# The low part of each mixer's last output chunk on VectorE, two reordered steps at the end of the RWKV mixer, and an arena 224 bytes lower

## Chip, core and metric

The kernel runs on one core of a Trainium2 chip. The metric is the device time of one launch in microseconds (us). The kernel before takes 1237.35 us (median of three runs, 1236.31 to 1237.88). Its profiled execution took 1236.65 us, of which 1234.8 us are the span that the profile covers.

The engines are named as in the profile: PE is TensorE, PEld its weight load, DVE is VectorE, ACT is ScalarE, POOL is GpSimd, SP issues the DMAs of the weights.

## What is computed

The reference is two transformer blocks on 256 tokens of width 1024, all in float32. Four SwiGLU feed-forward layers of width 2816 alternate with three mixers:

```python
x = x + 0.5 * swiglu(rmsnorm(x, ffn1_norm), gate, up, down)                # ffn 0
x = x + concat([spatial_gating(...), gated_delta_rule(...)]) @ w_out       # mix1
x = x + 0.5 * swiglu(rmsnorm(x, ffn2_norm), gate, up, down)                # ffn 1
x = rmsnorm(x, final_norm)
x = x + concat([forgetting_attention(...), causal_pool(...)]) @ hy_w_out   # fox
x = x + swiglu(rmsnorm(x), gate, up, down)                                 # ffn 2
x = x + (group_norm(rwkv7_scan(...)) + bonus) * g @ rw_w_o                 # rwkv
x = x + swiglu(rmsnorm(x), gate, up, down)                                 # ffn 3
```

Each mixer ends in a product of a 256 x 1024 activation with a 1024 x 1024 weight (`w_out`, `hy_w_out`, `rw_o`), added to the residual `x`. What follows is a feed-forward layer, whose first step is the norm of that sum.

## The kernel before

**Weights.** All weights come as a stream of chunks of 128 x 2048 float32 (1 MB each), in the order of their use. SP loads chunk c into `raw[:, c % 3]`. For products that are split in three, ScalarE rounds the chunk to `whi` (`high`, line 314) and GpSimd makes the rest, `wlo = raw - whi` (`low`, line 3371); both have three slots. TensorE then runs three passes of float32r products: high by high, high by low, low by high (`three_passes`, lines 341 to 346), or in the feed-forward layers one product of 512 columns and one of 256 (`ffn_tile`, lines 353 and 355). The semaphores are `high_made`, `low_made` (one more for each chunk) and `chunk_used`. `LOWS[c]` is the count that `low_made` has once the chunk c has its low part. GpSimd works through the lows strictly in the order of the stream, with a few other tasks in between.

**The arena.** Apart from the weights, `x` and constants, nearly everything lies in one buffer, `arena`; `f_both` (the feed-forward's activations, high and low), `hhi`, `hlo`, `key_hi`, `key_lo` are names for places in it. It starts behind a filler, `up_to_line`.

**The end of a mixer.** An output weight is four chunks of 256 columns. Chunks 0 and 1 are multiplied together (512 columns to a product, `pair_tiles`), then chunk 2 and chunk 3 alone in `last_out` (48 products of 256 columns each). Between them TensorE transposes pieces of the new `x` for the next norm (`turn_piece`, line 750). Chunk 3 can be rounded by ScalarE only when the pair is done, since it takes a slot that the pair used; its low part follows on GpSimd. VectorE adds the products to `x` in four steps (`add_out`, lines 1039 to 1045), and after the second has nothing to do until the first transposed piece has been rounded (`low_piece`, line 692).

**The end of the RWKV mixer.** Its output Y (kept where `x` was; `x` itself is saved in `kept_x` and comes back by DMA, line 2479) is finished in four passes w = 0 to 3, two token halves by two halves of the width. For each pass VectorE runs `normed(w)`, `whole(w)` (line 2755) and `gated(w)` (line 2764); TensorE transposes the result (`turned(w)`, line 3209); ScalarE rounds it to `hhi` (`y_high`, line 2475); VectorE makes `hlo` (`y_low(w)`, line 2770), which TensorE's `out_tiles(w)` waits for: 4 tiles by three passes, 12 products of 512 columns. The order of each engine is written out by hand. GpSimd makes the low part of `rw_o` chunk 2 only after the last `y_low` (it waits for `rw_ylo` at 4).

Of the kernel before, what the change touches and what calls it, by code (L numbers as in the profile page):

```python
# [20 lines left out]
P = 128  # L21
# [3 lines left out]
KT = D // P  # L25
# [3 lines left out]
RAW = 3  # L29
# [3 lines left out]
F32 = mybir.dt.float32  # L33
F32R = mybir.dt.float32r
ALU = mybir.AluOpType
# [158 lines left out]
def build(nc, stream, consts, vectors, x_in, rows, kept_x, out):  # L194
    names = stream_plan(STAGES)
    CH = {name: c for c, name in enumerate(names)}
# [14 lines left out]
    with ctx:  # L211
        def sb(name, shape, dt=F32):
            return ctx.enter_context(nc.sbuf_tensor(name, shape, dt))
# [12 lines left out]
        stat = sb("stat", [P, 64])  # L226
        sb("up_to_line", [P, 72])
        H_AT = 23040
# [456 lines left out]
        def pieces_vector(eng, n, stage, factor):  # L685
# [10 lines left out]
            def first_low(c, j):  # L696
# [4 lines left out]
                if j == 3:  # L701
                    eng.wait_ge(s("first_low"), 4 * c + 4)
                    nc.vector.tensor_copy(stat[:, 58:59], stat[:, 62:63]).then_inc(low_made, 1)

            for j in range(4):
                if stage:
                    add_out(eng, OUT_KIND[STAGES[stage - 1][0]], j)
                    if j:
                        low_piece(j - 1)
                else:  # L710
                    low_piece(j)
                    first_low(0, j)
# [333 lines left out]

        PAIR_BANKS = {"w_out": (3, 7), "hy_w_out": (6, 7), "rw_o": (5, 6)}
        LAST_BANKS = {"w_out": (6, 7), "hy_w_out": (0, 6), "rw_o": (0, 6)}

# [1474 lines left out]
        def rwkv_vector(eng, st):  # L2524
# [304 lines left out]
            normed(3)  # L2829
            whole(3)  # L2830
            y_low(2)
            gated(3)
            y_low(3)
            eng.wait_ge(s("x_kept"), 48)

        def rwkv_tensor(eng, st):
# [374 lines left out]

            def out_tiles(w):

                m, q = PASSES[w]
                eng.wait_ge(s("rw_ylo"), w + 1)
                return pair_tiles("rw_o", range(4 * q, 4 * q + 4), 0, m, last=KT - 1)

# [19 lines left out]
            out_tiles(0)  # L3237
            out_tiles(1)
            turned(2)
            turned(3)  # L3240
            out_tiles(2)
# [118 lines left out]
        def _(pool):  # L3360
# [13 lines left out]
            def lows_ffn(c0):  # L3374

                for c in range(c0, c0 + 3):
                    if c >= 2:
                        low(c)
                with pool.Fori(0, GROUPS - 1) as i:
                    for r in range(3):  # L3380
                        low(c0 + 3 + r, i)
# [3 lines left out]
            for st in STAGES:  # L3385
# [3 lines left out]
                while c < NCH and names[c][0] not in ("gate", "up", "down"):  # L3389
# [4 lines left out]
                    if c == CH[("rw_o", 0, 0)]:  # L3394
                        rwkv_pool(pool, low)
                    elif c not in PLAIN and names[c] not in (("lora", 0, 2), ("rw_o", 0, 1)):
                        low(c)
# [78 lines left out]
```

## Time and profile before

| | us |
|---|---|
| time, median of three runs | 1237.35 (1236.31 to 1237.88) |
| profiled execution | 1236.65 |
| its span | 1234.8 |
| PE busy | 1221.0 (99%) |
| POOL busy | 776.7 (63%) |
| ACT busy | 608.5 (49%) |
| DVE busy | 538.0 (44%) |

A row of a timeline gives the start and the length in us, the engine, the line, the operation, what it writes from what, and in brackets how long the engine had been idle before and what ended that. A product's length includes its way through the array, so the pace of TensorE is the distance between two starts, not the length.

### The profile page before, as it was taken

Reading aid. Unit: us, or ns where it says so; the run is one execution under the profiler, and the core shown is the slowest. Engines: PE = TensorE matmul, PEld = TensorE weight load, DVE = VectorE, ACT = ScalarE, POOL = GpSimd, SP = SyncE. Lnnn points to the kernel's source line nnn. Section 1 sums busy time; section 2 is a strip of 40 time slices with the busy share of each in tenths; the row PEclk is TensorE's granted clock in tenths of the full one; section 3 lists DMA queues with packets and bytes.
Section 4 is the critical chain, followed back from the end, with each engine's and each line's share of the span. In section 5 each row is a group of like instructions: output and inputs, shape, how many; then the busy total and the mean of one; then the engine's idle time right before and its main releaser. Section 6 shows DMA issues by size and latency. Waiting matters only on the chain.

```text
span 1234.8 us, 23237 instructions
## 1 busy us (share of the span) xinstructions
PE 1221.0 (99%) x9698; PEld 1062.6 (86%) x9698; DVE 538.0 (44%) x819; ACT 608.5 (49%) x796; POOL 776.7 (63%) x200
## 2 busy tenths in 40 slices
PE   8999999999999999999999999999999999999998
PEld 7888887788988888899898888888888998888887
DVE  4432234655333333343523333348986573332233
ACT  7454443545554444585565445464422444554442
POOL 3988880153288888767369888843016525888884
PEclk9999999999999999999999999999999999999999
DMA  8655554253255555554235555542341133555551
GB/s 301 212 186 199 178 201 148 89 184 140 103 174 201 202 175 200 193 184 160 103 137 202 176 201 179 195 170 103 136 163 44 38 117 122 184 195 197 180 201 68
DMA packets 31020, 202.01 MB, mean 164 GB/s; under 512 B 3424, under 2 KB 5344, under 8 KB 7392
## 3 DMA queue, kind: packets, MB, share of 16 engines
q1 hardware_dynamic: 28064, 196.63, 45.2%
q10 hardware_dynamic: 2880, 4.26, 1.0%
q8 instruction: 60, 0.98, 0.3%
q14 instruction: 16, 0.13, 0.0%
HBM read 198.79 MB, written 2.10 MB: 163 GB/s over the span
## 4 chain that ended last, share of the span: by engine, by line
PE 95%; ACT 1%; POOL 1%; issue 1%; DVE 1%; DMA 1%; SPq 0%; POOLq 0%; DVEq 0%; ACTq 0%
PE psum L353 25%; PE psum L355 13%; PE psum L344 10%; PE psum L346 10%; PE psum L345 10%; PE psum L986 6%; PE psum L999 3%; PE psum L2992 2%; PE psum L3008 1%; POOL wlo L3371 1%; PE psum L2847 1%; PE psum L341 1%; PE psum L343 1%; PE psum L342 1%; PE psum L2962 1%
## 5 line engine op out<-in xcount | busy, mean ns | idle before, releaser
L3371 POOL TENSOR_TENSOR wlo<-raw,whi 128x2048 fp32r<-128x2048 f32 x160 | 734.3, 4595 | 289.7 <-ACT whi L314 244.3
L353 PE MATMUL psum<-f_both,whi 128*128 128x512 f32 x1408 | 497.3, 394 | 1.0 <-DVE wlo L699 1.0
L314 ACT ACTIVATE whi<-raw 128x2048 fp32r<-128x2048 f32 x160 | 306.3, 1915 | 223.1 <-PE psum L355 173.9
L355 PE MATMUL psum<-f_both,wlo 128*128 128x256 f32 x1408 | 397.4, 282 | 0.0
L353 PEld LDWEIGHTS psum<-f_both,whi 128*128 128x128 f32 x1408 | 264.4, 188 | 62.0 <-DVE wlo L699 1.6
L355 PEld LDWEIGHTS psum<-f_both,wlo 128*128 128x128 f32 x1408 | 264.7, 188 | 1.5
L344 PE MATMUL psum<-whi,ahi 128*128 128x512 f32 x352 | 137.2, 390 | 0.2 <-POOL wlo L3371 0.2
L346 PE MATMUL psum<-whi,alo 128*128 128x512 f32 x352 | 137.0, 389 | 0.0
L345 PE MATMUL psum<-wlo,ahi 128*128 128x512 f32 x352 | 137.0, 389 | 0.0
L909 DVE TENSOR_TENSOR psum<-psum,arena 128x512 f32<-128x512 f32 x43 | 30.1, 700 | 239.7 <-ACT arena L625 239.6
L925 DVE TENSOR_TENSOR alo<-arena,ahi 128x512 fp32r<-128x512 f32 x44 | 98.7, 2244 | 31.7 <-ACT ahi L858 31.7
L916 DVE TENSOR_TENSOR psum<-psum,arena 128x512 f32<-128x512 f32 x44 | 30.8, 700 | 174.5 <-ACT arena L625 174.5
L344 PE MATMUL psum<-whi,hhi 128*128 128x256 f32 (+1 forms) x328 | 100.1, 305 | 0.4 <-POOL wlo L3371 0.2
L346 PE MATMUL psum<-whi,hlo 128*128 128x256 f32 (+1 forms) x328 | 97.4, 297 | 0.0
L345 PE MATMUL psum<-wlo,hhi 128*128 128x256 f32 (+1 forms) x328 | 97.4, 297 | 0.0
L344 PEld LDWEIGHTS psum<-whi,ahi 128*128 128x128 f32 x352 | 66.1, 188 | 14.5 <-POOL wlo L3371 0.5
L346 PEld LDWEIGHTS psum<-whi,alo 128*128 128x128 f32 x352 | 66.0, 188 | 13.7
L345 PEld LDWEIGHTS psum<-wlo,ahi 128*128 128x128 f32 x352 | 66.1, 188 | 12.2
L986 PE MATMUL psum<-arena,raw 128*128 128x256 f32 x320 | 73.9, 384 | 0.8 <-issue 0.8
L986 PEld LDWEIGHTS psum<-arena,raw 128*128 128x128 f32 x320 | 59.3, 190 | 10.4 <-issue 2.7
L344 PEld LDWEIGHTS psum<-whi,hhi 128*128 128x128 f32 x328 | 62.0, 189 | 4.6 <-issue 1.6
L345 PEld LDWEIGHTS psum<-wlo,hhi 128*128 128x128 f32 x328 | 62.2, 190 | 1.9
(425 smaller groups left out, 1474.1 us busy)
## 6 DMA issues: line engine op xcount, KB each, us to landing
raw<-stream SPq DMA_DIRECT2D x182, 1024.0 KB, 4.8
con<-consts SPq DMA_DIRECT2D x1, 1376.0 KB, 14.2
x<-x_in SPq DMA_DIRECT2D x1, 1024.0 KB, 4.9
raw<-stream SPq DMA_DIRECT2D x2, 512.0 KB, 6.9
kept_x<-x ACTq DMA_DIRECT2D x1, 1024.0 KB, 3.9
x<-kept_x ACTq DMA_DIRECT2D x2, 512.0 KB, 4.7
out<-x SPq DMA_DIRECT2D x4, 256.0 KB, 2.0
arena<-gm_w_s ACTq DMA_DIRECT2D x1, 512.0 KB
```

The source lines that it names most:

```text
L314: nc.scalar.activation(whi[:, slot, :], raw[:, c % RAW, :], ACT.Copy).then_inc(high_made, 1)
L344: nc.tensor.matmul(out, h_hi, w_hi, start=start, stop=False, skip_group_check=skip)
L345: nc.tensor.matmul(out, h_hi, w_lo, start=False, stop=False, skip_group_check=skip)
L346: return nc.tensor.matmul(out, h_lo, w_hi, start=False, stop=stop, skip_group_check=skip)
L353: nc.tensor.matmul(psum[:, bank, :].rearrange("p (a n) -> p a n", a=2), whi[w], f_both[:, :, k, :], start=k == 0, stop=False, skip_group_c ...
L355: return nc.tensor.matmul(psum[:, bank, 0:TOK], wlo[w], f_hi[:, k, :], start=False, stop=k == KT - 1, skip_group_check=True)
L909: nc.vector.tensor_tensor(left, left, aside[:, 0, :, :], ALU.add).then_inc(s("ffn_sum"), 1)
L916: nc.vector.tensor_tensor(left, left, aside[:, 1, :, :], ALU.add).then_inc(s("ffn_sum"), 1)
L925: nc.vector.tensor_tensor(flat(alo), act[:, b, :], flat(ahi).bitcast(F32), ALU.subtract)\
L986: mm = nc.tensor.matmul(psum[:, bank, j * 256:(j + 1) * 256], raw[:, slot, k * 256 + j * P:k * 256 + j * P + P], h[:, k, :], start=k == 0, ...
L999: mm = nc.tensor.matmul(psum[:, bank, m * 256:m * 256 + n], h[:, k, m * P:m * P + P], raw[:, slot, k * 256:k * 256 + n], start=k == 0, sto ...
L3371: nc.gpsimd.tensor_tensor(part(wlo[:, slot, :]), part(raw[:, c % RAW, :]), part(whi[:, slot, :]).bitcast(F32), ALU.subtract)\
```

## The change

There are three parts.

1. The filler before the arena has 16 columns instead of 72. The arena, and all that lies in it, starts 56 x 4 = 224 bytes lower in each partition: at byte 103968 instead of 104192. 104192 is 407 x 256; 103968 is 406 x 256 + 32. What lies before the filler stays where it was.
2. The low part of chunk 3 of `w_out`, `hy_w_out` and `rw_o` is made by VectorE (`last_out_low`), between the second and the third residual addition. GpSimd leaves these three out, and before its first low of the feed-forward layer that follows it waits until `low_made` has counted VectorE's. It waits in the first feed-forward layer for nothing.
3. At the end of the RWKV mixer `gated(3)` stands ahead of `y_low(2)` on VectorE, and `turned(2)` stands in the middle of `out_tiles(1)` on TensorE instead of behind it.

```diff
--- before.py
+++ after.py
@@ -224,7 +224,7 @@
         con = sb("con", [P, CONSTS.shape[1]])
         vec = sb("vec", [P, VEC_COLS])
         stat = sb("stat", [P, 64])
-        sb("up_to_line", [P, 72])
+        sb("up_to_line", [P, 16])
         H_AT = 23040
         MORE_AT = H_AT + 2 * KT * TOK
         ARENA = MORE_AT + 3072
@@ -702,9 +702,18 @@
                     eng.wait_ge(s("first_low"), 4 * c + 4)
                     nc.vector.tensor_copy(stat[:, 58:59], stat[:, 62:63]).then_inc(low_made, 1)
 
+            def last_out_low(c):
+                slot = SLOT[c]
+                eng.wait_ge(high_made, LOWS[c] - 2)
+                eng.wait_ge(low_made, LOWS[c] - 1)
+                nc.vector.tensor_tensor(wlo[:, slot, :], raw[:, c % RAW, :], whi[:, slot, :].bitcast(F32), ALU.subtract)\
+                    .then_inc(low_made, 1)
+
             for j in range(4):
                 if stage:
                     add_out(eng, OUT_KIND[STAGES[stage - 1][0]], j)
+                    if j == 1:
+                        last_out_low(CH[(OUT_KIND[STAGES[stage - 1][0]], 0, 3)])
                     if j:
                         low_piece(j - 1)
                 else:
@@ -1045,6 +1054,7 @@
                 nc.vector.tensor_tensor(xs, xs, bank2(LAST_BANKS[kind][j - 2]), ALU.add).then_inc(x_ready, 1)
 
         PAIR_BANKS = {"w_out": (3, 7), "hy_w_out": (6, 7), "rw_o": (5, 6)}
+        LAST_CHUNKS = [(kind, 0, 3) for kind in ("w_out", "hy_w_out", "rw_o")]
         LAST_BANKS = {"w_out": (6, 7), "hy_w_out": (0, 6), "rw_o": (0, 6)}
 
         def pair_slots(kind):
@@ -2828,8 +2838,8 @@
             gated(2)
             normed(3)
             whole(3)
+            gated(3)
             y_low(2)
-            gated(3)
             y_low(3)
             eng.wait_ge(s("x_kept"), 48)
 
@@ -3209,11 +3219,11 @@
                     mm = nc.tensor.transpose(bank4(GATE_BANK[w])[:, k, :], Y[:, m, (4 * q + k) * P:(4 * q + k + 1) * P], const("ident"))
                 mm.then_inc(s("rw_out"), 1)
 
-            def out_tiles(w):
+            def out_tiles(w, tiles=range(4)):
 
                 m, q = PASSES[w]
                 eng.wait_ge(s("rw_ylo"), w + 1)
-                return pair_tiles("rw_o", range(4 * q, 4 * q + 4), 0, m, last=KT - 1)
+                return pair_tiles("rw_o", [4 * q + k for k in tiles], 0, m, last=KT - 1)
 
             u_from_state(2)
             state_and_next_values(2)
@@ -3235,8 +3245,9 @@
             for j in range(2):
                 eng.wait_ge(low_made, LOWS[CH[("rw_o", 0, j)]])
             out_tiles(0)
-            out_tiles(1)
+            out_tiles(1, (0, 1))
             turned(2)
+            out_tiles(1, (2, 3))
             turned(3)
             out_tiles(2)
             out_tiles(3).then_inc(chunk_used, 2)
@@ -3373,6 +3384,8 @@
 
             def lows_ffn(c0):
 
+                if c0:
+                    pool.wait_ge(low_made, LOWS[c0] - 1)
                 for c in range(c0, c0 + 3):
                     if c >= 2:
                         low(c)
@@ -3393,7 +3406,7 @@
                         mix1_pool(pool, (3,))
                     if c == CH[("rw_o", 0, 0)]:
                         rwkv_pool(pool, low)
-                    elif c not in PLAIN and names[c] not in (("lora", 0, 2), ("rw_o", 0, 1)):
+                    elif c not in PLAIN and names[c] not in (("lora", 0, 2), ("rw_o", 0, 1)) and names[c] not in LAST_CHUNKS:
                         low(c)
                     c += 1
 
```

VectorE at the end of the RWKV mixer, before (line 2755 is `whole`, 2764 `gated`, 2770 `y_low`, 1039 and 1045 `add_out`, 692 `low_piece`):

```order
L2751 TENSOR_TENSOR x<-x,arena 128x512
L2755 TENSOR_TENSOR x<-x,arena 128x512
L2770 TENSOR_TENSOR hlo<-psum,hhi 128x4x128
L2764 TENSOR_TENSOR x<-x,psum 128x512
L2770 TENSOR_TENSOR hlo<-psum,hhi 128x4x128
L1039 TENSOR_TENSOR x<-x,psum 128x2x256 x2
L692 SCALAR_TENSOR_TENSOR f_both<-psum,vec,f_both 128x256 x2
L1045 TENSOR_TENSOR x<-x,psum 128x2x256
```

and after (ten lines further down in the file: 2765, 2774, 2780; the new operation is line 709):

```order
L2761 TENSOR_TENSOR x<-x,arena 128x512
L2765 TENSOR_TENSOR x<-x,arena 128x512
L2774 TENSOR_TENSOR x<-x,psum 128x512
L2780 TENSOR_TENSOR hlo<-psum,hhi 128x4x128 x2
L1048 TENSOR_TENSOR x<-x,psum 128x2x256 x2
L709 TENSOR_TENSOR wlo<-raw,whi 128x2048
L692 SCALAR_TENSOR_TENSOR f_both<-psum,vec,f_both 128x256 x2
L1054 TENSOR_TENSOR x<-x,psum 128x2x256
```

The gating of the last pass has moved ahead of both remaining `y_low`, and the new `wlo<-raw,whi` stands between the additions of output chunks 0 and 1 and the first `low_piece`.

TensorE from the second tile of `out_tiles(1)` to the beginning of `out_tiles(2)`, before (lines 344 to 346 are the three passes of one tile; 3209 is `turned`, four transposes each):

```order
L344 MATMUL psum<-whi,hhi 128x512
L345 MATMUL psum<-wlo,hhi 128x512
L346 MATMUL psum<-whi,hlo 128x512
L344 MATMUL psum<-whi,hhi 128x512
L345 MATMUL psum<-wlo,hhi 128x512
L346 MATMUL psum<-whi,hlo 128x512
L3209 MATMUL psum<-con,x 128x128 x8
L344 MATMUL psum<-whi,hhi 128x512
```

and after (`turned` is line 3219):

```order
L344 MATMUL psum<-whi,hhi 128x512
L345 MATMUL psum<-wlo,hhi 128x512
L346 MATMUL psum<-whi,hlo 128x512
L3219 MATMUL psum<-con,x 128x128 x4
L344 MATMUL psum<-whi,hhi 128x512
L345 MATMUL psum<-wlo,hhi 128x512
L346 MATMUL psum<-whi,hlo 128x512
L344 MATMUL psum<-whi,hhi 128x512
L345 MATMUL psum<-wlo,hhi 128x512
L346 MATMUL psum<-whi,hlo 128x512
L3219 MATMUL psum<-con,x 128x128 x4
L344 MATMUL psum<-whi,hhi 128x512
```

The eight transposes stood together behind all four tiles of pass 1; now four of them, those of pass 2, have two tiles (six products) between them and those of pass 3.

VectorE at the end of mix1, where `w_out`'s additions are four narrower instructions (line 1042 before, 1051 after), after the change:

```order
L1547 TENSOR_TENSOR hlo<-arena,hhi 128x512
L1051 TENSOR_TENSOR x<-x,psum 128x256 x4
L709 TENSOR_TENSOR wlo<-raw,whi 128x2048
L692 SCALAR_TENSOR_TENSOR f_both<-psum,vec,f_both 128x256 x2
L1054 TENSOR_TENSOR x<-x,psum 128x2x256
```

The new operation has the same place there, as it has behind `hy_w_out`.

## Rows read from the trace of the kernel before

**Rows 1.** The page, first part: busy us (share of the span) xinstructions of each engine.

```profile
PE 1221.0 (99%) x9698; PEld 1062.6 (86%) x9698; DVE 538.0 (44%) x819; ACT 608.5 (49%) x796; POOL 776.7 (63%) x200
```

**Rows 2.** PE timeline, RWKV out_tiles(0) to the first product of chunk 2: start, length.

```profile
1018.14 0.48 PE L344 MATMUL psum<-whi,hhi 128*128 128x512 f32 x1
...
1023.81 0.60 PE L3209 MATMUL psum<-con,x 128*128 128x128 f32 x4
1026.48 0.66 PE L3209 MATMUL psum<-con,x 128*128 128x128 f32 x4 [2.08 <-DVE x L2764]
1026.90 0.47 PE L344 MATMUL psum<-whi,hhi 128*128 128x512 f32 x1
...
1034.12 0.28 PE L344 MATMUL psum<-whi,hhi 128*128 128x256 f32 x1
```

**Rows 3.** Window: us, busy (x) of PE, PEld, DVE, ACT, POOL; PEclk, DMA, GB/s.

```profile
1026.90:1034.12 7.22, 7.22 (x28) 5.76 (x26) 0.69 (x1) 0.69 (x2) 4.58 (x1) 0.76 0.24 75
```

**Rows 4.** DVE timeline at the same place.

```profile
1020.79 0.69 DVE L2764 TENSOR_TENSOR x<-x,psum 128x512 f32<-128x512 f32 x1
...
1022.35 0.69 DVE L2755 TENSOR_TENSOR x<-x,arena 128x512 f32<-128x512 f32 x1
1025.14 0.69 DVE L2770 TENSOR_TENSOR hlo<-psum,hhi 128x512 fp32r<-128x512 f32 x1 [2.11 <-ACT hhi L2475]
1025.75 0.68 DVE L2764 TENSOR_TENSOR x<-x,psum 128x512 f32<-128x512 f32 x1
```

**Rows 5.** ACT queue at the same place: the second half of x comes back.

```profile
1027.18 0.33 ACTq L2479 DMA_DIRECT2D x<-kept_x  x1
```

**Rows 6.** The line that brings x back: its DMAs from issue to landing.

```profile
DMA to landing us min/median/max: 4.6/4.7/4.8
```

**Rows 7.** POOL timeline, low parts of rw_o chunks 2 and 3.

```profile
1028.65 4.58 POOL L3371 TENSOR_TENSOR wlo<-raw,whi 128x2048 fp32r<-128x2048 f32 x1 [28.50 <-DVE hlo L2770]
1036.39 4.59 POOL L3371 TENSOR_TENSOR wlo<-raw,whi 128x2048 fp32r<-128x2048 f32 x1 [3.17 <-ACT whi L314]
```

**Rows 8.** PE timeline around the start of rw_o chunk 3.

```profile
1039.82 1.03 PE L750 MATMUL psum<-con,x 128*128 128x128 f32 x8
1041.04 0.39 PE L344 MATMUL psum<-whi,hhi 128*128 128x256 f32 x1 [0.18 <-POOL wlo L3371]
```

**Rows 9.** DVE timeline, additions of rw_o chunks 0 and 1.

```profile
1034.38 1.29 DVE L1039 TENSOR_TENSOR x<-x,psum 128x512 f32<-128x512 f32 x2 [5.88 <-PE psum L346]
```

**Rows 10.** Line 2628, a low part made by VectorE: ns, min/median/max.

```profile
L2628 DVE TENSOR_TENSOR wlo<-raw,whi x1: 1212/1212/1212, 913.2 to 913.2; 128x1024 fp32r<-128x1024 f32 x1
```

**Rows 11.** Groups by line: shapes, count, busy us, mean ns of one, idle before.

```profile
L925 DVE TENSOR_TENSOR alo<-arena,ahi 128x512 fp32r<-128x512 f32 x44 | 98.7, 2244 | 31.7 <-ACT ahi L858 31.7
```

**Rows 12.** PE timeline, end of hy_w_out chunk 2 and start of chunk 3.

```profile
632.22 1.03 PE L750 MATMUL psum<-con,x 128*128 128x128 f32 x8
633.01 0.37 PE L344 MATMUL psum<-whi,hhi 128*128 128x256 f32 x1
```

**Rows 13.** POOL timeline at that place: low of hy_w_out chunk 3.

```profile
627.36 4.61 POOL L3371 TENSOR_TENSOR wlo<-raw,whi 128x2048 fp32r<-128x2048 f32 x1 [3.18 <-ACT whi L314]
```

**Rows 14.** DVE timeline there: additions of hy_w_out chunks 0 and 1.

```profile
626.73 1.28 DVE L1039 TENSOR_TENSOR x<-x,psum 128x512 f32<-128x512 f32 x2 [9.64 <-PE psum L346]
```

**Rows 15.** PE timeline in the first feed-forward layer: a wait, then full clock.

```profile
10.17 0.50 PE L353 MATMUL psum<-f_both,whi 128*128 128x512 f32 x1 [1.04 <-DVE wlo L699]
```

**Rows 16.** The window around it, all engines, columns as in rows 3.

```profile
9.00:15.00 6.00, 4.96 (x28) 4.13 (x28) 5.76 (x13) 6.00 (x14) 0.00 (x0) 1.00 1.03 437
```

**Rows 17.** Groups by line of PE: products streamed from the arena and from whi.

```profile
L353 PE MATMUL psum<-f_both,whi 128*128 128x512 f32 x1408 | 497.3, 394 | 1.0 <-DVE wlo L699 1.0
...
L344 PE MATMUL psum<-whi,ahi 128*128 128x512 f32 x352 | 137.2, 390 | 0.2 <-POOL wlo L3371 0.2
...
L345 PE MATMUL psum<-wlo,hhi 128*128 128x256 f32 x288 | 81.0, 281 | 0.0
...
L342 PE MATMUL psum<-hlo,whi 128*128 128x256 f32 x48 | 13.5, 282 | 0.0
```

## The prediction

> **What bounds the kernel now.** I read the first part of the page first: TensorE is busy 1221.0 us, 99% of the span, and no other engine is above 63% [rows 1]. So an edit on VectorE or GpSimd is worth only what TensorE waits for it, and the question for each of the three parts is whether TensorE waits at that place. I then read TensorE's timeline at the ends of the three mixers, which the change touches, and the timelines of VectorE, ScalarE and GpSimd beside it.
>
> There is one wait worth speaking of. In the RWKV mixer TensorE finishes `out_tiles(1)` and `turned(2)`, which starts at 1023.81, and then stands idle for 2.08 us until `turned(3)` starts at 1026.48; VectorE's line 2764, the gating, ended it [rows 2]. VectorE's timeline says why: `whole(3)` starts at 1022.35 and takes 0.69, and `gated(3)` could follow at once, but `y_low(2)` stands ahead of it in the queue and waits for ScalarE until 1025.14; `gated(3)` runs at 1025.75 [rows 4]. TensorE thus waits for something that stands behind an operation which needs TensorE's own last result.
>
> This wait has a second price. `out_tiles(0)` and `out_tiles(1)`, 24 products, take 1023.81 - 1018.14 = 5.67 us. The same number in `out_tiles(2)` and `(3)` takes 1034.12 - 1026.90 = 7.22 us [rows 2]. In the window of those 7.22 us the granted clock is 0.76 on average [rows 3], so TensorE was for a part of it at 1.2 GHz instead of 2.4, after the idle stretch. That cost 7.22 - 5.67 = 1.55 us.
>
> A second, small wait is in front of `rw_o` chunk 3. TensorE starts eight transposes at 1039.82 and the chunk at 1041.04, on GpSimd's low part [rows 8]. At the end of `hy_w_out` the same eight transposes take 633.01 - 632.22 = 0.79 us with no wait behind them [rows 12]. So 1.22 - 0.79 = 0.43 us were lost there.
>
> **The reordering (part 3), step by step.** `turned(2)` needs `gated(2)`, done at 1020.79 + 0.69 = 1021.48 [rows 4]. It now starts after 18 of the 24 products: 1018.14 + 18 x 0.236 = 1022.39, no wait. Four transposes take 0.42 (1026.48 to 1026.90). Six more products end at 1024.23. `gated(3)` now starts right behind `whole(3)`, 1022.35 + 0.72 = 1023.07, and is done by 1023.75, so `turned(3)` starts at 1024.23 without a wait, and `out_tiles(2)` could start at 1024.65. It needs `y_low(2)`. Before, `y_low(2)` started 1.33 after `turned(2)` (1023.81 to 1025.14), ScalarE's rounding included; now that gives 1022.39 + 1.33 = 1023.72, and `gated(3)` is out of VectorE's way by then; it ends at 1024.41, 0.24 before it is wanted. So the 2.08 us go, and `out_tiles(2)` starts at 1024.65 instead of 1026.90: 2.25 us. If the clock stays up, the 24 products take 5.67 and end at 1030.32 instead of 1034.12: 3.80 us in all.
>
> What is late next is GpSimd. Its low part of `rw_o` chunk 2 starts only after the last `y_low`; before, that was 1028.65, 2.17 after `turned(3)`, and it took 4.58 [rows 2, 7]. Now 1024.23 + 2.17 = 1026.40, done at 1030.98, seen by TensorE some 0.05 later, as with chunk 3 (1036.39 + 4.59 = 1040.98 against 1041.04 [rows 7, 8]). TensorE arrives at 1030.32 and waits 0.7 us, until 1031.03. Of the 3.80 us 3.09 stay.
>
> The saved `x` comes back by a DMA that is issued behind the last rounding, at 1027.18, 0.70 after `turned(3)` [rows 5]; it takes up to 4.8 us [rows 6]. Now it is issued at 1024.93 and lands by 1029.7. VectorE's first addition comes 0.26 after the pair's last product (1034.38 against 1034.12 [rows 2, 9]), now 1030.58. It is not late.
>
> **The low part of chunk 3 on VectorE (part 2).** The trace has the same operation on VectorE at half the width, 1.21 us for 1024 columns [rows 10], so I take 2.4 us for 2048, against 4.6 on GpSimd [rows 7]. In the RWKV mixer ScalarE's rounding was ready when GpSimd began, 1036.39 - 1034.12 = 2.27 after the pair; now 1032.59. The two additions, 1.29 us [rows 9], are done at 1031.87. So the low part is ready at about 1035.0. TensorE wants it at 1031.03 + 5.70 (chunk 2, 1034.12 to 1039.82) + 0.79 = 1037.52. The wait of 0.43 us is gone, with 2.5 us to spare.
>
> At `hy_w_out` nothing was waited for before, so nothing can be won. The rounding is ready at 627.36 [rows 13], the additions end at 626.73 + 1.28 = 628.01 [rows 14], the low part would be ready at 630.4, and TensorE wants it at 633.01 [rows 12]. It is behind 2.6 us of slack. `w_out` is laid out alike. Nothing: 0.
>
> The operation stands on VectorE ahead of `low_piece(0)`, which waits for transposes that start only at 1039.82 [rows 8], 4.2 us after the additions are done (1034.38 + 1.29 [rows 9]); these idle microseconds hide it. GpSimd's new wait holds back the low of the first feed-forward chunk; what is queued behind it there is only the feed-forward's lows. Before, that chunk had to wait for GpSimd's 4.6 us of chunk 3 anyway; VectorE is done earlier than that, so the new wait costs nothing as long as VectorE takes under 4.6 us.
>
> VectorE and GpSimd do disturb each other here. Line 925 reads two operands from the arena and `ahi` and takes 2244 ns for 512 columns [rows 11], while the half-chunk above took 1212 ns for 1024 [rows 10]. The Trainium skill, page "SBUF — State Buffer", section "Who interferes with whom", says that a VectorE instruction with two SBUF inputs and a GpSimd instruction that reads SBUF exclude each other for their whole length; the slow row fits it. It would speak against moving this very kind of operation to VectorE. Its result is a rival below.
>
> **The arena (part 1).** No row of before shows a product that streams from an address 32 bytes past a multiple of 64, so its cost has to be bounded. The products that stream from `f_both` in the arena take 394 ns each, 1408 of them; those that stream as many columns from `whi`, outside it, 390 [rows 17]. If the place of the start were behind these 4 ns, the move could give them back or cost as much again: 1408 x 4 ns = 5.6 us either way. The other pair says that it does not matter: 256 columns streamed from `hlo` in the arena take 282 ns, from `wlo` outside it 281 [rows 17], at different distances from a multiple of 256. That is the nearer pair, since it differs in the place alone; I take 0. The Trainium skill, same page, section "Operand start alignment", asks only for a multiple of the element's size, and says that this is about what is allowed and that nothing was timed; it leaves the sum as it is.
>
> **The sum.** 3.09 + 0.43 + 0 + 0 = 3.52 us. The profiled execution takes 1236.65, of which 1234.8 are the span; with the change it would be 1233.1. The median of the runs shown is 0.70 above the profiled one, so I predict 1237.35 - 3.5 = 1233.8 us. Its own range, from waits of some tenths at the splits, is 1233.0 to 1234.9.
>
> **Rivals.**
> 1. *The new wait for GpSimd takes the clock down as the old one did.* For it: TensorE still stands for 0.7 us before chunk 2. Against: in the first feed-forward layer TensorE stood for 1.04 us [rows 15] and the granted clock around it is 1.00 [rows 16]. It would cost the 1.55 us again: 1235.3. Chance 8%.
> 2. *The arena's place slows the streaming products.* A mechanism of its own: a start off a line costs each of the 1408 pairs of products something. From 2.5 ns on it eats the gain; at 4 ns, 5.6 us, the time is 1239.4, slower than before; to be slower by more than can be told it takes 4.3 ns. For it: lines 353 and 344 do differ by 4 ns. Against: the pair of 281 and 282 ns. 16%.
> 3. *The arena's place makes them faster.* The same 4 ns won: 1228.2. For and against as above. 10%.
> 4. *VectorE's low part meets GpSimd.* If it ran at the pace of line 925, 4 x 2.24 = 9.0 us, it would end at 1032.59 + 9.0 = 1041.6, 4.1 us after TensorE wants it, and at 628.01 + 9.0 = 637.0, 4.0 us late, at `w_out` about the same: 12 us lost against 3.5 won, 1246. It decides from about 5 us on. This is what the rule on the shared port would do. Against: GpSimd's next low waits on this very operation, and its low of chunk 2 ends (1030.98) before the rounding is ready (1032.59). 3%.
> 5. *The reordering does not bring what it says*: `y_low(2)` becomes the thing that is late, since it now stands behind `gated(3)`, and TensorE stands for it instead; if the 2.08 us and the slow clock only moved there, the 0.43 us would be all that is won: 1236.9. Against: the 0.24 us of slack worked out above. 3%.
>
> The forecast has 60%. A measurement of this kernel tells about 0.2% from no change, 2.5 us; 3.5 is not far above it, so I count one in eight of the forecast as "same". Faster: 0.53 of the forecast and 0.09 of rival 3, 0.62. Slower: 0.08 of rival 2, 0.03 of rival 4 and 0.03 for what I do not see, 0.14. Same: the rest, 0.24. The range is 1230.0 to 1239.0: it leaves out the far halves of rivals 2 and 3, and rival 4.
>
> **What would show it.** In the profile after: TensorE's wait on the gating gone, and a new one of 0.3 to 1.0 us on GpSimd's line before `rw_o` chunk 2; four transposes after 18 products; 24 products of `out_tiles(2)` and `(3)` in about 5.7 us at a granted clock of 1.00; VectorE's low part three times at 2.2 to 2.6 us, and no wait before chunk 3. Lines 353 and 355 with the same mean and the feed-forward layers of the same length would show that the arena's place is nothing. The prediction is wrong if these layers change in length, if the clock falls again, or if VectorE's new operation takes over 4.6 us.

## The result: 1229.66 us, and the profile after

The changed kernel takes 1229.66 us (median of six runs, 1229.11 to 1231.06), the kernel before 1236.76 beside it (six runs, 1235.15 to 1237.88). The ratio is 0.9944, with a 95% interval of 0.9931 to 0.9957. That is 7.1 us, twice the 3.5 of the forecast and below its range, which ended at 1230.0. The profiled execution of the changed kernel has a span of 1227.9 us against 1234.8.

I cut both traces at the first and the last product of line 353 of each feed-forward layer. The distances between these rows, after minus before:

| stretch | before | after | difference |
|---|---|---|---|
| start to the first product of ffn 0 | 10.17 | 10.62 | +0.45 |
| ffn 0 | 174.46 | 173.47 | -0.99 |
| mix1 | 157.68 | 158.49 | +0.81 |
| ffn 1, 2 and 3, each | 173.03 | 171.78 | -1.25 (-3.75 for the three) |
| fox | 123.81 | 124.28 | +0.47 |
| rwkv | 235.01 | 231.06 | -3.95 |

They sum to -6.96; the spans differ by 6.9. The feed-forward layers gave 4.74 us that were not forecast, and inside them the change moves nothing but the address of their operand. Of the RWKV mixer's 3.95 us, 3.34 lie behind the first product of `out_tiles(0)`: from there to the first product of ffn 3 it is 1041.48 - 1015.77 = 25.71 us instead of 1047.19 - 1018.14 = 29.05, near the forecast. The other 0.6 us lie ahead of it, in a part where profiles differ by up to 2.4 us without any rule that I could find.

**The end of the RWKV mixer.** TensorE's timeline after the change, from the first product of `out_tiles(0)` to the start of chunk 3 (the lines are the same as in [rows 2, 8]; `turned` is 3219 now and `turn_piece` 759):

```profile
1015.77 0.47 PE L344 MATMUL psum<-whi,hhi 128*128 128x512 f32 x1
...
1020.05 0.60 PE L3219 MATMUL psum<-con,x 128*128 128x128 f32 x4
...
1021.89 0.60 PE L3219 MATMUL psum<-con,x 128*128 128x128 f32 x4
1022.24 0.48 PE L344 MATMUL psum<-whi,hhi 128*128 128x512 f32 x1
...
1027.69 0.39 PE L346 MATMUL psum<-whi,hlo 128*128 128x512 f32 x1
1028.65 0.39 PE L344 MATMUL psum<-whi,hhi 128*128 128x256 f32 x1 [0.56 <-POOL wlo L3382]
...
1034.51 1.03 PE L759 MATMUL psum<-con,x 128*128 128x128 f32 x8
1035.30 0.36 PE L344 MATMUL psum<-whi,hhi 128*128 128x256 f32 x1
```

Read the distances from the first row: `turned(2)` comes 4.28 behind it (forecast 4.25), `turned(3)` 6.12 (6.09), `out_tiles(2)` 6.47 (6.51), chunk 2 12.88 (12.89), and chunk 3 another 6.65 behind chunk 2 (6.49). No wait stands at either `turned`. The one that is left is on GpSimd, before chunk 2: 0.56 us. The window of that stretch (columns as in [rows 3]) shows that the clock stayed up:

```profile
1017.65:1028.65 11.00, 10.44 (x50) 8.13 (x49) 5.38 (x10) 2.45 (x5) 4.60 (x1) 1.00 0.15 49
```

VectorE's timeline at the same place shows the gating (2774) straight behind `whole` (2765), both `y_low` (2780) behind it, and the new low part (709):

```profile
1019.98 0.69 DVE L2765 TENSOR_TENSOR x<-x,arena 128x512 f32<-128x512 f32 x1
1020.70 0.69 DVE L2774 TENSOR_TENSOR x<-x,psum 128x512 f32<-128x512 f32 x1
1021.32 0.69 DVE L2780 TENSOR_TENSOR hlo<-psum,hhi 128x512 fp32r<-128x512 f32 x1
1023.16 0.69 DVE L2780 TENSOR_TENSOR hlo<-psum,hhi 128x512 fp32r<-128x512 f32 x1 [1.14 <-ACT hhi L2485]
1028.19 1.28 DVE L1048 TENSOR_TENSOR x<-x,psum 128x512 f32<-128x512 f32 x2 [4.34 <-PE psum L346]
1030.15 2.29 DVE L709 TENSOR_TENSOR wlo<-raw,whi 128x2048 fp32r<-128x2048 f32 x1 [0.68 <-ACT whi L314]
```

The low part takes 2.29 us and is done at 1032.44; TensorE wants it at 1035.30. GpSimd, one operation shorter, does these two here:

```profile
1023.99 4.60 POOL L3382 TENSOR_TENSOR wlo<-raw,whi 128x2048 fp32r<-128x2048 f32 x1 [26.77 <-DVE hlo L2780]
1032.86 4.62 POOL L3382 TENSOR_TENSOR wlo<-raw,whi 128x2048 fp32r<-128x2048 f32 x1 [4.27 <-ACT whi L314]
```

**The feed-forward layers.** The groups of TensorE by line, of the changed kernel, which answer to [rows 17]:

```profile
L353 PE MATMUL psum<-f_both,whi 128*128 128x512 f32 x1408 | 492.2, 393 | 1.9 <-DVE wlo L699 1.9
L355 PE MATMUL psum<-f_both,wlo 128*128 128x256 f32 x1408 | 393.7, 280 | 0.0
L344 PE MATMUL psum<-whi,ahi 128*128 128x512 f32 x352 | 137.4, 390 | 0.3 <-POOL wlo L3382 0.3
...
L345 PE MATMUL psum<-wlo,hhi 128*128 128x256 f32 x288 | 81.0, 281 | 0.0
```

The same view of the kernel before has this for line 355:

```profile
L355 PE MATMUL psum<-f_both,wlo 128*128 128x256 f32 x1408 | 397.4, 282 | 0.0
```

The mean lengths moved by 1 or 2 ns, and the products of lines 344 and 345 did not move. It is the pace that tells. Eight neighbouring products of line 353 in ffn 1, before:

```profile
512.18 0.40 PE L353 MATMUL psum<-f_both,whi 128*128 128x512 f32 x1
512.41 0.28 PE L355 MATMUL psum<-f_both,wlo 128*128 128x256 f32 x1
...
514.64 0.39 PE L353 MATMUL psum<-f_both,whi 128*128 128x512 f32 x1
...
515.34 0.40 PE L353 MATMUL psum<-f_both,whi 128*128 128x512 f32 x1
```

and after, where the first row is that of the layer's first product:

```profile
342.58 0.48 PE L353 MATMUL psum<-f_both,whi 128*128 128x512 f32 x1
...
511.93 0.39 PE L353 MATMUL psum<-f_both,whi 128*128 128x512 f32 x1
512.16 0.28 PE L355 MATMUL psum<-f_both,wlo 128*128 128x256 f32 x1
...
514.36 0.39 PE L353 MATMUL psum<-f_both,whi 128*128 128x512 f32 x1
```

Seven pairs of products take 514.64 - 512.18 = 2.46 us before and 514.36 - 511.93 = 2.43 after. Over all pairs the mean from the start of a 353 to that of its 355 fell from 230.7 to 229.5 ns, and from a 355 to the next 353 from 120.0 to 117.5: 3.7 ns a pair. 1408 pairs times 3.7 ns is 5.2 us; the layers lost 4.7. The last rows of the two fences are the last products of the layer: 515.34 - 342.31 (its first, before) = 173.03 and 514.36 - 342.58 = 171.78.

So two questions were open: is it the arena that does this, by what property of its address, and what are the other two parts worth by themselves?

### The profile page after: what moved, and what is told of

Its sections match the earlier page's. It is cut to its first block, busy times and chain, and to the rows that moved or that the text cites. A ratio compares the mean times of both kernels' runs of the same rounds, so it can differ in the third digit from the quotient of the medians.

```text
span 1227.9 us, 23243 instructions
## 1 busy us (share of the span) xinstructions
PE 1214.9 (99%) x9698; PEld 1059.2 (86%) x9698; DVE 540.9 (44%) x822; ACT 608.6 (50%) x796; POOL 765.3 (62%) x197
## 4 chain that ended last, share of the span: by engine, by line
PE 95%; ACT 1%; POOL 1%; issue 1%; DVE 1%; DMA 1%; SPq 0%; POOLq 0%; DVEq 0%
PE psum L353 25%; PE psum L355 13%; PE psum L344 10%; PE psum L346 10%; PE psum L345 10%; PE psum L995 6%; PE psum L1008 3%; PE psum L3002 2%; PE psum L3018 1%; POOL wlo L3382 1%; PE psum L2857 1%; PE psum L341 1%; PE psum L342 1%; PE psum L343 1%; PE psum L2972 1%
## 5 line engine op out<-in xcount | busy, mean ns | idle before, releaser
L3382 POOL TENSOR_TENSOR wlo<-raw,whi 128x2048 fp32r<-128x2048 f32 (+1 forms) x157 | 722.9, 4608 | 295.5 <-ACT whi L314 210.0
L353 PE MATMUL psum<-f_both,whi 128*128 128x512 f32 x1408 | 492.2, 393 | 1.9 <-DVE wlo L699 1.9
L355 PE MATMUL psum<-f_both,wlo 128*128 128x256 f32 x1408 | 393.7, 280 | 0.0
L934 DVE TENSOR_TENSOR alo<-arena,ahi 128x512 fp32r<-128x512 f32 x44 | 94.4, 2146 | 31.7 <-ACT ahi L867 31.7
L867 ACT ACTIVATE ahi<-arena 128x512 fp32r<-128x512 f32 x44 | 27.9, 633 | 73.8 <-DVE arena L931 73.8
```

Source lines behind the costliest of these rows:

```text
L353: nc.tensor.matmul(psum[:, bank, :].rearrange("p (a n) -> p a n", a=2), whi[w], f_both[:, :, k, :], start=k == 0, stop=False, skip_group_c ...
L355: return nc.tensor.matmul(psum[:, bank, 0:TOK], wlo[w], f_hi[:, k, :], start=False, stop=k == KT - 1, skip_group_check=True)
L934: nc.vector.tensor_tensor(flat(alo), act[:, b, :], flat(ahi).bitcast(F32), ALU.subtract)\
L3382: nc.gpsimd.tensor_tensor(part(wlo[:, slot, :]), part(raw[:, c % RAW, :]), part(whi[:, slot, :]).bitcast(F32), ALU.subtract)\
```

## The three parts, each by itself

**The arena alone.** The kernel before with one number changed:

```diff
-        sb("up_to_line", [P, 72])
+        sb("up_to_line", [P, 16])
```

> Part 1 alone: the filler has 16 columns, all else as before. Theory A (the arena's place sets the pace of the products that stream from it): the feed-forward layers shorten from 173.03 us to 171.78 us each, as in the changed kernel, 4.7 to 5 us in all; mix1 and fox lengthen by 0.8 and 0.5 us if their lengthening is the place's too; the time is 3.5 us under before. Theory B (the place is nothing, and the layers are shorter because GpSimd and VectorE share the work in another way): the layers stay at 173.03 and the time stays within 0.5 us of before.

Measured: 1232.68 us, ratio 0.9972 (0.9962 to 0.9983). This and the next three runs are compared with the kernel before as it ran beside them, 1236.36 us. The layers take 173.48 once and 171.78 three times, as in the changed kernel (173.47 and 171.78); the groups of lines 353 and 355 read 492.2 and 393.7 us, as there. The arena is the cause in the feed-forward layers, and it is worth 0.28% in all, 3.5 us. Fox gave back 0.5 us of it: 124.31 here against 123.81 before, and 123.81 to 123.95 in the next three runs, which have the old arena. Mix1's 157.93 is not the arena's doing: the next two runs have 157.90 and 157.94 with the arena where it was (before 157.68).

This run showed something on the side. The old wait at `turned(3)` is there, and the clock did not fall. Its timeline of TensorE and the window behind the wait:

```profile
1024.93 0.66 PE L3209 MATMUL psum<-con,x 128*128 128x128 f32 x4 [2.08 <-DVE x L2764]
1025.35 0.48 PE L344 MATMUL psum<-whi,hhi 128*128 128x512 f32 x1
...
1031.76 0.39 PE L344 MATMUL psum<-whi,hhi 128*128 128x256 f32 x1 [0.56 <-POOL wlo L3371]
```

```profile
1024.00:1031.00 7.00, 6.07 (x28) 4.82 (x28) 1.57 (x3) 0.69 (x2) 3.91 (x1) 1.00 0.22 77
```

The same 2.08 us as in [rows 2], but a granted clock of 1.00 behind it instead of 0.76 [rows 3]; and TensorE, not slowed, met the wait on GpSimd that the slow stretch had hidden. Chunk 2 starts 15.17 us behind the first product of `out_tiles(0)`, against 15.97 before. The fallen clock cost 0.80 us at the end, not 1.55.

**The reordering alone** (`gated(3)` ahead of `y_low(2)`, and `turned(2)` after two of the four tiles):

```diff
-            y_low(2)
             gated(3)
+            y_low(2)
...
-            out_tiles(1)
+            out_tiles(1, (0, 1))
             turned(2)
+            out_tiles(1, (2, 3))
```

> Part 3 alone: gated(3) ahead of y_low(2), turned(2) in the middle of out_tiles(1); filler 72, low parts all on GpSimd. By the forecast's steps 3.1 us less: the wait of 2.08 us and the slow clock gone, a wait of 0.6 to 0.7 us for GpSimd before rw_o chunk 2, and the small wait before chunk 3 (0.43 us) still there or changed by some tenths. Feed-forward layers at 173.03. Rival: the reordering gives the whole gain of 7 us; then the layers would be at 171.78 here.

Measured: 1233.83 us, ratio 0.9978 (0.9969 to 0.9987): 0.22% of 1236.36, 2.7 us. Chunk 2 starts 12.84 behind the first product, 3.13 sooner than before and 2.33 sooner than in the run with the clock up. GpSimd and TensorE at chunk 3:

```profile
1034.26 13.75 POOL L3372 TENSOR_TENSOR wlo<-raw,whi 128x2048 fp32r<-128x2048 f32 x3 [1.61 <-ACT whi L314]
```

```profile
1038.57 1.04 PE L750 MATMUL psum<-con,x 128*128 128x128 f32 x8
1039.36 0.37 PE L344 MATMUL psum<-whi,hhi 128*128 128x256 f32 x1
```

The first of the three lows is that of chunk 3: 1034.26 + 4.6 = 1038.9, before TensorE arrives at 1039.36. The 0.43 us of [rows 8, 12] is gone with the reordering alone: TensorE, made to wait for GpSimd before chunk 2, does not meet it again before chunk 3.

**VectorE's low part alone** (`last_out_low` and its wait in `lows_ffn`, as in the diff of the change; order and filler as before):

```diff
                     add_out(eng, OUT_KIND[STAGES[stage - 1][0]], j)
+                    if j == 1:
+                        last_out_low(CH[(OUT_KIND[STAGES[stage - 1][0]], 0, 3)])
```

> Part 2 alone: chunk 3's low part on VectorE in all three mixers, filler 72, order as before. Forecast: 0.4 us less, from the wait before rw_o chunk 3, nothing elsewhere. Theory B expects the feed-forward layers at 171.78 and 3 to 4 us less. If the lengthening of mix1 (0.8) and fox (0.5) comes from VectorE's operation, it is seen here.

Measured: 1236.78 us, ratio 1.0003 (0.9994 to 1.0012). Nothing. In its profile the wait before chunk 3 is gone (6.48 us from chunk 2 to chunk 3, against 6.92), and the clock had fallen again behind the old wait:

```profile
1027.69 0.66 PE L3219 MATMUL psum<-con,x 128*128 128x128 f32 x4 [2.08 <-DVE x L2774]
1028.10 0.47 PE L344 MATMUL psum<-whi,hhi 128*128 128x512 f32 x1
```

```profile
1028.10:1035.30 7.20, 7.20 (x27) 5.73 (x26) 0.69 (x1) 0.69 (x2) 4.58 (x1) 0.76 0.22 75
```

0.44 us is 0.04% and lies inside the interval; and in a run where the clock stays up, as with the arena alone, TensorE meets GpSimd before chunk 2 and its trace has no wait before chunk 3 that could be removed.

**Both of these without the arena** (the changed kernel with the old filler):

```diff
-        sb("up_to_line", [P, 16])
+        sb("up_to_line", [P, 72])
```

> Parts 2 and 3 together, filler 72: what the forecast spoke of apart from the arena. By its sum 3.5 us less than before, with layers at 173.03. Theory A: so, and 3.5 us slower than the changed kernel. Theory B: as fast as the changed kernel.

Measured: 1233.65 us, ratio 0.9981 (0.9972 to 0.9990). The RWKV mixer takes 231.06 us, to the hundredth as in the changed kernel, and the three later layers 173.03, as before. VectorE's low part adds nothing to the reordering (0.9981 with it, 0.9978 without). The ratios of the parts, 0.9981 and 0.9972, multiply to 0.9953; the changed kernel has 0.9944, within the intervals.

## Which property of the address

The start of the arena moved from a multiple of 256 to 32 past one; `whi` and `wlo`, which stand ahead of the filler, start at 128 past one in both. I moved the arena on, with the rest of the changed kernel as it is. All four differ in one number:

```diff
-        sb("up_to_line", [P, 16])
+        sb("up_to_line", [P, N])       # N = 80, 40, 24, 32
```

**N = 80: byte 104224**, another address with the same remainder, 32.

> The changed kernel with filler 80: arena at 104224, which is 407 x 256 + 32. Theory A1 (what counts is the place modulo 256, or modulo 64: 32 bytes past): feed-forward layers of 171.78 us, time as the changed kernel. Theory A2 (what counts is the distance to whi and wlo in whole, or the absolute place): another length.

Measured: 1230.05 us, ratio 0.9948 (0.9931 to 0.9965), layers of 171.78: the changed kernel over again. The remainder counts, not the address.

**N = 40: byte 104064**, 128 past a multiple of 256, like the weights.

> The changed kernel with filler 40: arena at 104064, 406 x 256 + 128, a multiple of 64 and the same remainder by 256 as raw, whi and wlo. Theory A1a (a start off a multiple of 64 is what helps): 173.03 us for a layer, as at 104192. Theory A1b (what hurts or helps is the remainder by 256 against that of the weights): neither 173.03 nor 171.78.

Measured: 1239.06 us, ratio 1.0019 (1.0009 to 1.0028), layers of 174.00. With the arena here, the whole change would have made the kernel slower.

**N = 24: byte 104000**, 64 past.

> The changed kernel with filler 24: arena at 104000, 406 x 256 + 64, a multiple of 64. Theory A1a: 173.03 us for a layer. Theory A1b: a third value. If it is 171.78 too, only the exact multiple of 256 is bad.

Measured: 1236.3 us, ratio 0.9998 (0.9988 to 1.0008), layers of 174.15. The group of line 353 here:

```profile
L353 PE MATMUL psum<-f_both,whi 128*128 128x512 f32 x1408 | 500.8, 398 | 1.4 <-DVE wlo L699 1.4
```

**N = 32: byte 104032**, 96 past.

> The changed kernel with filler 32: arena at 104032, 406 x 256 + 96, which is 32 past a multiple of 64, as at 103968. Theory A1a: 171.78 us for a layer. Theory A1b: a third value.

Measured: 1230.2 us, ratio 0.9946 (0.9929 to 0.9962), layers of 172.35, but shorter mixers than in the changed kernel (157.61 and 123.11).

So a multiple of 64 is not the good place (64 and 128 past are the worst), and 32 bytes decide over 6 us. This left two theories: it is the place of the streamed operand by itself, or its distance from the weights that stand in the array. The next two kernels move the weights too.

**Weights and arena both 32 bytes higher than in the kernel before.** The weights are at 160 past, the arena at 32 past, where it was fast; the distance is the 128 of the kernel before, with which it was slow.

```diff
+        sb("ahead", [P, 8])
         ...
-        sb("up_to_line", [P, 16])
+        sb("up_to_line", [P, 72])
```

> The changed kernel with 32 bytes of filler ahead of raw, and filler 72: the weights (raw, whi, wlo, ahi, alo), x and the constants 32 bytes higher, at 160 past a multiple of 256 instead of 128; arena at 104224, 32 past. All distances between operands are those of the kernel with filler 72. Theory R (the distance between the streamed operand and the weights counts): layers of 173.03 us. Theory S (the streamed operand's own place counts): the pace of the products from f_both as at 103968, 171.78 for the layer, or a little off it where the down products, which stream from whi and wlo, change their pace of 226.8 ns.

Measured: 1232.97 us, ratio 0.9972 (0.9960 to 0.9984), layers of 173.03. Its groups (the lines are one further down), and its first and last product of ffn 1:

```profile
L354 PE MATMUL psum<-f_both,whi 128*128 128x512 f32 x1408 | 497.2, 394 | 1.6 <-DVE wlo L700 1.6
L356 PE MATMUL psum<-f_both,wlo 128*128 128x256 f32 x1408 | 397.4, 282 | 0.0
```

```profile
342.83 0.48 PE L354 MATMUL psum<-f_both,whi 128*128 128x512 f32 x1
...
515.85 0.40 PE L354 MATMUL psum<-f_both,whi 128*128 128x512 f32 x1
```

497.2 and 397.4 are the values of the kernel before (497.3 and 397.4), not the 492.2 and 393.7 that the arena had with the same remainder. So the place of `f_both` by itself does not count, but its distance from what lies ahead of the filler. `raw`, `whi`, `wlo`, `ahi`, `alo`, `x` and the constants moved together here. That it is the distance from `whi` and `wlo`, the other operands of these products, is the likely reading; no run moves these two alone.

**The weights alone 32 bytes higher, and the arena where it was before** (104192): the distance is 96.

```diff
+        sb("ahead", [P, 8])
         ...
-        sb("up_to_line", [P, 16])
+        sb("up_to_line", [P, 64])
```

> As the run before, but arena at 104192, a multiple of 256, with the weights at 160 past. Theory R: the distance is that of arena 104160 with the weights in their old place, so the layer is as long as there. Theory S: lines 353 and 355 as in the kernel before, 230.7 and 120.0 ns apart; the down products (whi, wlo streamed) may change.

Measured: 1234.35 us, ratio 0.9979 (0.9970 to 0.9988), layers of 173.16. Beside it ran the same distance made the other way, **the weights where they were and the arena at 104160**:

```diff
-        sb("up_to_line", [P, 16])
+        sb("up_to_line", [P, 64])
```

> The changed kernel with filler 64: arena at 104160, 406 x 256 + 224. Odd multiples of 32 bytes gave 171.78 and 172.35 us for a layer, multiples of 64 gave 173.03 to 174.15. If that is the rule, this one is under 172.5. It is also the pair of the run before for theory R.

Measured: 1234.22 us, ratio 0.9979 (0.9970 to 0.9989), layers of 173.16. The other rule in its expectation, that odd multiples of 32 bytes are fast, fails with this: it asked for less than 172.5. Two kernels whose operands lie at different places, with the same distance, have the same layers to the hundredth of a microsecond. All that ran with the changed code, by the distance from the weights up to `f_both`, modulo 256 (the weights standing for all that lies ahead of the filler):

| distance | kernels | a feed-forward layer | start to start, 353 / 355 (ns) | ratio |
|---|---|---|---|---|
| 160 | after; N = 80 | 171.78 | 229.5 / 117.5 | 0.9944; 0.9948 |
| 224 | N = 32 | 172.35 | 230.2 / 118.1 | 0.9946 |
| 128 | old filler; both higher | 173.03 | 230.7 / 120.0 | 0.9981; 0.9972 |
| 96 | weights higher; N = 64 | 173.16 | 232.3 / 118.3; 232.4 / 117.9 | 0.9979; 0.9979 |
| 0 | N = 40 | 174.00 | 235.4 / 116.7 | 1.0019 |
| 192 | N = 24 | 174.15 | 234.7 / 118.4 | 0.9998 |

Distances of 32 and 64 were not tried.

**A kernel from it.** `f_both` is streamed in the feed-forward layers; in the mixers it is the weights that are streamed, against `hhi` and `hlo` in the rest of the arena. The mixers were shortest where the arena was 64 past (157.21 and 122.61), the layers where it was 32 past. A filler of 8 columns behind `f_both`, and one ahead of the rest, gives each its own place: `f_both` at 103968, the rest at 104000.

```diff
+            below.enter_context(nc.sbuf_tensor("behind_f", [P, 8], F32))
...
+        sb("before_arena", [P, 8])
```

> The changed kernel with the two halves of the arena's use apart: f_both at byte 103968 (32 past a multiple of 256) as in the changed kernel, and all else of the arena, hhi, hlo and the keys too, 32 bytes higher at 104000 (64 past). Theory A1b (each streaming operand has its own pace by its own place): feed-forward layers at 171.78 us as at 103968, and mix1 and fox as short as with the whole arena at 104000, 157.2 and 122.6 us instead of 158.5 and 124.3; the time 3 us under the changed kernel, near 1227. Rival: the mixers' length has another source (the weights' last pieces, the loads); then the time is that of the changed kernel.

Measured: 1227.26 us (1225.66 to 1228.67), ratio 0.9921 (0.9907 to 0.9935). The groups that matter:

```profile
L355 PE MATMUL psum<-f_both,whi 128*128 128x512 f32 x1408 | 492.2, 393 | 2.1 <-DVE wlo L701 2.1
L357 PE MATMUL psum<-f_both,wlo 128*128 128x256 f32 x1408 | 393.7, 280 | 0.0
...
L347 PE MATMUL psum<-wlo,hhi 128*128 128x256 f32 x288 | 80.3, 279 | 0.0
```

The layers are those of the changed kernel (171.78), though the rest of the arena lies where the whole arena gave 174.15; so it is the place of `f_both`, and of nothing else in the arena, that sets them. The mixers' products of 256 columns fell from 281 to 279 ns; mix1 takes 157.47 instead of 158.49, fox 122.61 instead of 124.28, and the RWKV mixer 232.48 instead of 231.06. That loss lies ahead of `out_tiles(0)`, which takes 207.0 instead of 205.4 us, in the part that differs between profiles anyway. It is the fastest kernel here, 9.3 us below the kernel before. It did not run beside the changed kernel, and the two intervals overlap (0.9907 to 0.9935, and 0.9931 to 0.9957), so by how much it beats that one is less sure: 2.4 us by the medians.

## Why the prediction was wrong

**The step that failed is the arena term, "I take 0".** It was bounded by 1408 x 4 ns = 5.6 us either way, and the measured value is near the end of these bounds: 4.7 us in the layers, 3.5 us in all when the arena moves alone. I chose the middle because 256 columns took 281 ns from one place and 282 from another [rows 17]. Two things were wrong with that pair. It compares lengths, and the first part of this document says that the pace of TensorE is the distance between two starts; between before and after the mean length of line 353 moved 1 ns where the pair of products gained 3.7. And it does not differ "in the place alone": line 345 streams `wlo` against `hhi`, line 342 `hlo` against `whi`. `hhi` and `hlo` start whole multiples of 256 bytes into the arena, so with the arena at a multiple of 256 and the weights at 128 past one, both pairs of operands lie 128 apart modulo 256. The two groups have the same distance, and their agreement says nothing about another one. In place of the 0 the runs showed 3.7 ns less for each pair of products, at a distance of 160 instead of 128.

**Rival 3 came to 1228.2 for a wrong reason.** It had 10%, and its time is 1.5 us from the result. But its price was the 4 ns between lines 353 and 344. Afterwards these stand at 393 and 390, so the gap has hardly closed. The gain came from the pace, and two thirds of it from line 355, which the rival did not name.

**Rival 2 was real too.** At distances of 0 and 192 the same code lost, against the old filler, 0.0038 and 0.0017 of the ratio, 4.7 and 2.1 us. Both signs that the bounds held open exist, and 32 bytes are enough to go from one to the other. With nothing known about the rule, the honest range was the whole of the bounds, 1228.2 to 1239.4; mine cut 1.8 us off its lower half.

**The reordering: right in the profile.** 3.09 us were forecast before chunk 2, and the changed kernel shows 15.97 - 12.88 = 3.09. Each start on the way was within 0.04 us, the new wait on GpSimd came (0.56 us idle, forecast 0.7), and the clock stood at 1.00. The `x` that comes back was issued 6.76 behind the first product (forecast 6.79) and landed within 4.0 us, not late. Rivals 1 and 5 did not happen: in all eleven profiles with the new order the wait on GpSimd before chunk 2 is there, 0.55 to 0.68 us, and in none did the clock fall behind it.

**But the base was one profile.** The slow stretch in [rows 3] happens in some executions of this code and not in others: it is in the profiles of the kernel before and of the kernel with VectorE's low alone, and not in the one with the arena alone, with the same 2.08 us of idleness ahead of it in all three. Without it the reordering is worth 15.17 - 12.84 = 2.33 us. The timed runs gave 2.7 for it alone and 2.3 with VectorE's low (0.0022 and 0.0019 of 1236.36), between the two, though the interval of the first, 1.6 to 3.8 us, holds the 3.1 as well.

The granted clock of each timed run says how often the clock fell. One stretch of 3.41 us at half speed brings the mean over a run down to 0.999. Of 73 runs of the kernel before, 29 have 1.0 and took 1235.98 us in the mean; 31 have 0.999 and took 1236.67, 0.7 us more, near the 0.80 above; 13 have 0.998 or 0.997. Of the 82 runs beside them with the new order, 64 have 1.0. So the old wait did not always bring the clock down: from 29 of 73 and 64 of 82, if all other falls are equally frequent in both, it did so in about half of the runs (an estimate). Then the reordering is worth 2.33 + 0.4 = 2.7 us, which is what was timed.

**VectorE's low part: its own duration right, its gain counted twice.** It took 2.29 us (2.4 forecast), in all three mixers, and ended 2.9 us before it was wanted (2.5 forecast). But the 0.43 us was no longer there to be won. The prediction's own numbers say it: after the reordering ScalarE's rounding is ready at 1032.59, so GpSimd would have been done at 1032.59 + 4.59 = 1037.18, and TensorE wants the chunk at 1037.52. I took the wait out of the old timeline after I had moved everything in it. Rival 4 did not happen, but was not put to the test either: GpSimd was idle each time that the low part ran. The three occurrences in the changed kernel, by the view of that line:

```profile
L709 DVE TENSOR_TENSOR wlo<-raw,whi x3: 2285/2287/2292, 331.4 to 1030.2; 128x2048 fp32r<-128x2048 f32 x3
```

**The price of rival 4 was misread.** It took the 2244 ns of line 925 [rows 11] for a pace. In the trace of before they are a wait; here is the operation once during a low of GpSimd and once with GpSimd idle:

```profile
170.58 4.61 POOL L3371 TENSOR_TENSOR wlo<-raw,whi 128x2048 fp32r<-128x2048 f32 x1 [0.99 <-ACT whi L314]
173.33 2.42 DVE L925 TENSOR_TENSOR alo<-arena,ahi 128x512 fp32r<-128x512 f32 x1 [0.70 <-ACT ahi L858]
...
188.12 0.69 DVE L925 TENSOR_TENSOR alo<-arena,ahi 128x512 fp32r<-128x512 f32 x1 [0.70 <-ACT ahi L858]
```

Alone it takes 0.69 us. Begun during the low, which ends at 175.19, it ends at 175.75; 36 of the 44 occurrences go like that, and end 0.55 to 0.67 us behind the low. So VectorE's low part, had it begun with one of GpSimd's, would have cost at most about 4.6 + 2.3 = 6.9 us (an estimate from these rows), not 9.0.

**Summed up:** 3.52 forecast for the RWKV mixer's end, and 29.05 - 25.71 = 3.34 seen there in the profile, 3.09 of it ahead of chunk 2, and 2.3 to 2.7 in the timed runs; 0 forecast for the arena, and 3.5 to 4.6 timed (the arena alone; 0.9981 to 0.9944).

## What to carry to other kernels

When a change moves a buffer that TensorE streams, look at the pace, from one start to the next, over a whole layer, and not at the mean length of a product; a difference of 4 ns between two groups is 5 us when there are 1408 pairs. Where no row shows the new place, keep the full bounds in the range, and look at both operands of a product: two groups that agree may simply have the same distance between them. And before a wait is counted as won, move everything else in the timeline first: an earlier edit may have removed it.

## What the runs showed of the hardware

**The pace of the feed-forward layers' first products (lines 353 and 355, float32r) depends on the distance, modulo 256 bytes, between the streamed `f_both` and the block in which the weights lie.** A feed-forward layer of 352 pairs went from 171.78 to 174.15 us with it, 1.4%. It moved both paces, and not together: at a distance of 0 the 512-column product took 235.4 ns and the 256-column one 116.7, at 128 it was 230.7 and 120.0. The Trainium skill, page "SBUF — State Buffer", section "Who interferes with whom", gives TensorE two independent read ports, one for the moving operand and one for the weight load, and names the pair shared by VectorE and GpSimd as the only contention. Read so, no address should matter to TensorE; but between these kernels nothing but addresses changed, and the time did. The measurement decides. Whether the load of the next weights disturbs the stream is not shown; the runs give the times by address for this pair of products, not what lies beneath them. They do not carry over to other products: `whi` and `ahi` start with the same remainder, and the down products that stream one against the other (512 columns, distance 0) settle at 226.7 ns in every profile, faster than any in the table.

**The clock after an idle stretch is not settled by the stretch.** After the same 2.08 us the granted clock stood at half (1.2 GHz instead of 2.4) for 3.41 us in two profiles and at full speed in a third. A single profile is not enough to price it; the granted clocks of the timed runs were (29 of 73 runs at 1.0 with the old order, 64 of 82 with the new).

**A VectorE operation that reads two tensors from SBUF waits for a running GpSimd operation of that kind.** `alo<-arena,ahi` took 0.69 us alone and 2.42 us when it began 1.86 us before the end of a GpSimd low (the rows above).

**Left open:** the distances of 32 and 64; which of the tensors ahead of the filler `f_both` must be seen from; and why the down products are slower just behind the products from `f_both`. These come mostly in groups of 24. With the arena at 104064 the first ten of a group are 232.6 ns apart in the mean (227.0 before), though neither of their operands lies in the arena; from the eleventh on it is 226.7 in both kernels. Open is also the rest of the RWKV mixer, ahead of `out_tiles(0)`, which took 205.1 to 207.5 us in the profiles with no pattern that I could find.
